# A gate unit of 512 outputs by 512 inputs in a two-layer hybrid decoder kernel

## What is computed

```python
h = rms_norm(x, norm1_g[l]) * (1.0 + sc1) + sh1
proj = h @ w_in[l]
z, xbc, dt_raw, q, k, v, gate_s, gate_a = split_cols(proj, IN_PROJ_WIDTHS)   # z: 2048 columns
# mamba2_branch: causal conv and silu of xbc, chunked scan -> y (512 tokens, 4 groups of 512)
y = y.reshape(bsz, s, SSM_D_INNER) * jax.nn.silu(z.astype(jnp.float32))
yg = y.reshape(bsz, s, SSM_GROUPS, SSM_D_INNER // SSM_GROUPS)
yg = yg * lax.rsqrt(jnp.mean(yg * yg, axis=-1, keepdims=True) + EPS)
y_ssm = (yg.reshape(...) * norm_g) @ w_ssm_out[l]
y_att = diff_attention_branch(q, k, v, ...) @ w_attn_out[l]
x = x + g1 * ((sigmoid(gate_s) * y_ssm + sigmoid(gate_a) * y_att) @ w_out[l])
x = x + g2 * (square(relu(h2 @ w_ff1[l])) @ w_ff2[l])
```

## Time and profile before

| | us |
|---|---|
| median of three runs | 2360.05 (2359.25 to 2361.26) |
| the profiled execution, its own time | 2360.11 |
| its span, first to last instruction | 2358.3 |
| TensorE matmuls busy | 2285.5 |
| VectorE busy | 1368.7 |
| ScalarE busy | 1015.1 |
| GpSimd busy | 1109.9 |

### The profile page before, as it was taken

The page is one execution under the profiler, slowest core; times in us unless marked ns, Lnnn a source line. Parts: engine busy times, 40 slices in busy tenths (PEclk is TensorE's granted clock), DMA queues, the critical chain, the costliest instruction groups (busy, mean ns, idle before and its releaser), DMA issues.

```text
span 2358.3 us, 32040 instructions
## 1 busy us (share of the span) xinstructions
PE 2285.5 (97%) x11800; PEld 1910.3 (81%) x11800; DVE 1368.7 (58%) x2041; ACT 1015.1 (43%) x1862; POOL 1109.9 (47%) x825
## 2 busy tenths in 40 slices
PE   7999998999999989999989999999999998999997
PEld 6888996887778868888878889988878786888886
DVE  7678775466653567777847777613666434321324
ACT  2566642355553232322335666533556433332322
POOL 1465643544444444444435656544444444544442
PEclk9999999999999989999999999999999998999999
DMA  6333324522224335545423333232222232233321
GB/s 253 109 95 125 103 86 155 187 78 72 71 74 153 110 131 185 189 168 204 158 92 100 118 107 108 86 98 95 71 66 70 81 116 81 99 99 98 98 94 51
DMA packets 94125, 267.19 MB, mean 113 GB/s; under 512 B 8528, under 2 KB 35536, under 8 KB 88592
## 3 DMA queue, kind: packets, MB, share of 16 engines
q1 hardware_dynamic: 84656, 248.22, 31.2%
q10 hardware_dynamic: 9312, 16.91, 2.5%
HBM read 260.77 MB, written 4.33 MB: 112 GB/s over the span
## 4 chain that ended last, share of the span: by engine, by line
PE 49%; issue 23%; POOL 10%; POOLq 10%; DVE 3%; DVEq 1%; DMA 1%; PEld 1%; ACT 1%; ACTq 1%; SPq 0%; PEldq 0%
POOL w_lo L1808 10%; PE gemm L560 10%; PE gemm L562 10%; PE gemm L561 10%; POOLq L1810 10%; PE gemm L584 3%; PE gemm L583 3%; PE gemm L585 3%; PE aux L625 2%; PE aux L804 2%; PE aux L734 2%; PE aux L842 1%; PE aux L748 1%; PE aux L743 1%; DMA ada_pe<-stream 1%
## 5 line engine op out<-in xcount | busy, mean ns | idle before, releaser
L1808 POOL TENSOR_TENSOR w_lo<-raw,w_hi 128x512 fp32r<-128x512 f32 x704 | 978.2, 1410 | 1095.3 <-ACT w_hi L934 1087.3
L934 ACT ACTIVATE w_hi<-raw 128x1024 fp32r<-128x1024 f32 x352 | 371.3, 1058 | 719.9 <-PE gemm L562 606.1
L560 PE MATMUL gemm<-h_hi,w_hi 128*128 128x512 f32 x1504 | 604.6, 402 | 5.5 <-DVE h_lo L1374 4.9
L562 PE MATMUL gemm<-h_hi,w_lo 128*128 128x512 f32 x1504 | 589.4, 392 | 0.0
L561 PE MATMUL gemm<-h_lo,w_hi 128*128 128x512 f32 x1504 | 588.4, 391 | 0.0
L560 PEld LDWEIGHTS gemm<-h_hi,w_hi 128*128 128x128 f32 x1504 | 284.5, 189 | 64.7 <-issue 9.8
L562 PEld LDWEIGHTS gemm<-h_hi,w_lo 128*128 128x128 f32 x1504 | 283.7, 189 | 61.6
L561 PEld LDWEIGHTS gemm<-h_lo,w_hi 128*128 128x128 f32 x1504 | 284.6, 189 | 57.7 <-issue 1.9
L560 PE MATMUL gemm<-op_hi,w_hi 128*128 128x512 f32 x608 | 238.6, 392 | 0.2
L562 PE MATMUL gemm<-op_hi,w_lo 128*128 128x512 f32 x608 | 236.9, 390 | 0.0
L561 PE MATMUL gemm<-op_lo,w_hi 128*128 128x512 f32 x608 | 236.7, 389 | 0.0
(11 more groups left out here) (191 smaller groups left out, 3324.5 us busy)
## 6 DMA issues: line engine op xcount, KB each, us to landing
raw<-stream SPq DMA_DIRECT2D x336, 512.0 KB
ada_late<-stream SPq DMA_DIRECT2D x30, 1024.0 KB, 4.8
seg<-decay_rows ACTq DMA_DIRECT2D x64, 256.0 KB, 3.3
ada_early<-stream SPq DMA_DIRECT2D x40, 256.0 KB, 3.9
raw<-stream SPq DMA_DIRECT2D x32, 256.0 KB
ada_first<-stream SPq DMA_DIRECT2D x5, 1024.0 KB, 20.0
x<-xT SPq DMA_DIRECT2D x2, 2048.0 KB, 10.2
ada_pe<-stream SPq DMA_DIRECT2D x3, 1024.0 KB, 14.1
```

The costliest lines, as they stand in the source:

```text
L560: mm(o, w_hi[:, slot, k, cols], hi[:, k, :], start=k == 0, stop=False)
L562: last = mm(o, w_lo[:, slot, k, cols], hi[:, k, :], start=False, stop=k == KB - 1)
L934: A(w_hi[:, slot, ks], raw[:, slot, ks], ACT.Copy).then_inc(hi_ready, 1)
L1808: gp.tensor_tensor(w_lo[:, slot, ks], raw[:, slot, ks], w_hi[:, slot, ks].bitcast(F32), ALU.subtract)
```

## The change

A gate unit becomes 512 outputs by 512 inputs. Two in a row, the early (even) and the late (odd) one, cover a group's 512 outputs and all 1024 inputs, and token block t of the group accumulates in bank t through both. A part is two k-blocks by three products, 6 matmuls of 512 columns. TensorE signals token blocks 0 to 2 with `z_done` after parts 4 to 6 of the late unit and block 3 with the unit's end. Before part 2 of the early unit it waits for banks 2 and 3 as well. ScalarE makes one tanh of a bank for each token block into one of two `zt` buffers; VectorE multiplies (tanh + 1) by the bank itself, which frees it, and then by 0.5 and y. Both stand in the tick in which TensorE runs the token block's last part (`Z_AT`): ticks 22 (block 0) and 23 (three) for group 0, 27 and 28 (two each) for group 1, 33 (four) for group 2, 37 (four) for group 3. SyncE loads a half of such a unit with two transfers, two k-blocks of each of the two 256-column units in memory. The attention gate writes its temporary into `zt[:, 0]`, with the same size.

```diff
+PART_TICK = [_tick for _tick in range(T_FIRST, T_END) for _ in range(fill_of(_tick))]
+Z_AT = {}
+for _n in range(N_Z // 2 * TB):
+    Z_AT.setdefault(PART_TICK[KB * (U_Z + 2 * (_n // TB) + 1) + TB + _n % TB], []).append(divmod(_n, TB))
...
-        zt = place("zt", [P, 2, UW], F32, r_z)
-        zh = place("zh", [P, 2, UW], F32, r_z + T2)
+        zt = place("zt", [P, 2, S], F32, r_z)
...
+                elif U_Z <= n < U_O:
+
+                    rows = slice((n - U_Z) % 2 * TB + 2 * half, (n - U_Z) % 2 * TB + 2 * half + 2)
+                    for a in range(2):
+                        sp.dma_start(raw[:, slot, TB * half + a:TB * half + TB:2],
+                                     unit_of(l, place_of(n - (n - U_Z) % 2 + a))[:, rows]).then_inc(raw_in[slot][half], 16)
...
+            def gate_tokens(l, n, part):
+
+                slot, late = n % 2, (n - U_Z) % 2
+                half, t = divmod(part, TB)
+                o = gb[t][:]
+                toks = slice(t * P, (t + 1) * P)
+                if not late and part == 2:
+                    pe.wait_ge(bank_free[1], freed_at(l, n + 1) - 2)
+                for r in range(2 * half, 2 * half + 2):
+                    k = TB * late + r
+                    hi = w_hi[:, slot, 2 * r:2 * r + 2, :].rearrange("p a n -> p (a n)")
+                    lo = w_lo[:, slot, 2 * r:2 * r + 2, :].rearrange("p a n -> p (a n)")
+                    mm(o, h_hi[:, k, toks], hi, start=k == 0, stop=False)
+                    mm(o, h_lo[:, k, toks], hi, start=False, stop=False)
+                    last = mm(o, h_hi[:, k, toks], lo, start=False, stop=k == KB - 1)
+                if t == TB - 1:
+                    last.then_inc(gemm_done, 1)
+                elif late and half:
+                    last.then_inc(S_["z_done"], 1)
...
-                def tanh_z(n, j):
-                    act.wait_ge(gemm_done, done_at(l, n))
-
-                    act.wait_ge(S_["z_used"], mid_at(l, "z_used", 2 * (n - U_Z) + j) + Z_CREDIT)
-                    src = gb[2 * (n % 2) + j][:].rearrange("p (t n) -> p t n", t=2)
-                    A(zt[:], src, ACT.Tanh, scale=0.5)
-                    A(zh[:], src, ACT.Copy, scale=0.5).then_inc(bank_free[n % 2], 1)
-                    act.drain().then_inc(S_["z_act"], 1)
+                def tanh_z(g, t):
+                    if t < TB - 1:
+                        act.wait_ge(S_["z_done"], mid_at(l, "z_done", 3 * g + t) + 1)
+                    else:
+                        act.wait_ge(gemm_done, done_at(l, U_Z + 2 * g + 1))
+
+                    act.wait_ge(S_["z_used"], mid_at(l, "z_used", TB * g + t) - 1 + Z_CREDIT)
+                    A(zt[:, t % 2], gb[t][:], ACT.Tanh, scale=0.5).then_inc(S_["z_act"], 1)
...
-                def gate_y(n, j):
-
-                    g, u = divmod(n - U_Z, 2)
-                    dve.wait_ge(S_["z_act"], mid_at(l, "z_act", 2 * (n - U_Z) + j) + 1)
-                    STT(zt[:], zt[:], 1.0, zh[:], ALU.add, ALU.mult)
+                def gate_y(g, t):
+
+                    dve.wait_ge(S_["z_act"], mid_at(l, "z_act", TB * g + t) + 1)
+                    STT(zt[:, t % 2], zt[:, t % 2], 1.0, gb[t][:], ALU.add, ALU.mult).then_inc(bank_free[t // 2], 1)
                     settle()
-                    yv = y_tok[:, g, 2 * j:2 * j + 2, u * UW:(u + 1) * UW]
-                    TT(yv, yv, zt[:], ALU.mult)
+                    yv = y_tok[:, g, t, :]
+                    STT(yv, zt[:, t % 2], 0.5, yv, ALU.mult, ALU.mult)
                     dve.drain().then_inc(S_["z_used"], 1)
```

More of the change, by code:

```diff
@@ L170 @@
     ("mid", 1, {"seed": 24, "taps": 24, "tanh": 24, "silu": 24, "decay": 32, "m": 32, "m_used": 16, "xdt": 4, "xd": 4, "dx": 4, "state": 12,
-                "z_act": 16, "z_used": 16, "y_sq": 4, "y_ms": 4, "y_rs": 4, "yn": 16, "y_hi": 16, "y_lo": 16,
+                "z_done": 12, "z_act": 16, "z_used": 16, "y_sq": 4, "y_ms": 4, "y_rs": 4, "yn": 16, "y_hi": 16, "y_lo": 16,
                 "swap": 16, "rope": 16, "v": 4, "mx": 32, "e": 32, "p": 32, "pt": 32, "o_sq": 8, "o_ms": 8, "o_rs": 8,
@@ L371, in build @@
         LO_CREDIT, DONE_CREDIT, BANK_CREDIT, AUX_CREDIT, LAYER_CREDIT = 0, 4, 2, 1, 1
-        SILU_CREDIT, U_CREDIT, ROPE_CREDIT, Z_CREDIT, OUT_CREDIT, X_CREDIT = 4, 4, 2, 1, 2, KB
+        SILU_CREDIT, U_CREDIT, ROPE_CREDIT, Z_CREDIT, OUT_CREDIT, X_CREDIT = 4, 4, 2, 2, 2, KB
         GT_CREDIT = 2
@@ L696, in mid_part @@
                         open_half(l, n, k // (KB // 2))
-                    if U_Z <= n < U_O or n == U_Q + 2 or (U_AT <= n < U_AO and AT_UNITS[n - U_AT][0] == "v"):
+                    if U_Z <= n < U_O:
+                        gate_tokens(l, n, k)
+                    elif n == U_Q + 2 or (U_AT <= n < U_AO and AT_UNITS[n - U_AT][0] == "v"):
                         unit_tokens(n % 2, k)
@@ L1146, in act_program @@
                         exp_of_dt()
-                    for j in range(2):
-                        for n in since(tick, U_Z, U_O, 1 + j):
-                            tanh_z(n, j)
+                    for g, t in Z_AT.get(tick, ()):
+                        tanh_z(g, t)
                     for g in range(GROUPS):
@@ L1620, in dve_program @@
                         steps_of_dt()
-                    for j in range(2):
-                        for n in since(tick, U_Z, U_O, 1 + j):
-                            gate_y(n, j)
+                    for g, t in Z_AT.get(tick, ()):
+                        gate_y(g, t)
                     for g in range(GROUPS):
@@ L1723, in dve_program @@
                         dve.wait_ge(gemm_done, done_at(l, U_AO + u))
-                        STT(zt[:].rearrange("p a n -> p (a n)"), gate_a[:, 2 * u + j, :], 1.0, gb[c][:], ALU.add, ALU.mult)\
+                        STT(zt[:, 0], gate_a[:, 2 * u + j, :], 1.0, gb[c][:], ALU.add, ALU.mult)\
                             .then_inc(bank_free[u % 2], 1)
                         settle()
-                        TT(mix[:, 2 * u + j, :], mix[:, 2 * u + j, :], zt[:].rearrange("p a n -> p (a n)"), ALU.add)
+                        TT(mix[:, 2 * u + j, :], mix[:, 2 * u + j, :], zt[:, 0], ALU.add)
                         dve.drain().then_inc(S_["mixed"], 1)
```

## The result

The changed kernel takes 2375.14 us (median of 4 runs, 2373.23 to 2376.02) against 2360.02 us before (4 runs, 2359.25 to 2361.26): ratio 1.0062, 95% interval 1.0045 to 1.0080, 15.1 us slower. The forecast was 2367, slower, with a range up to 2377: the sign and the main term held, and the size was less than half of what came.

A forecast was written before the change was run, and what follows sets the result against it. TensorE's stream, without slack, was taken to set the end. Columns -10.0, banks +12.4, clock +3.7, gate +5.0 and first-layer chain -4.2 sum to +6.9 us on 2360.11: 2367.0 us, range 2357 to 2377.

The forecast's parts named there:

- What bounds the kernel: From first conv unit to last y turn TensorE sets the end; a new wait there is paid in full.
- The columns, -10.0: Gate-stage parts of six 512-column matmuls replace twelve of 256: 0.078 us less per part, 128 parts, -10.0 us.
- an estimate of 2 us: Gain for the columns from the skill page's isolated-matmul formula, in place of 10; the prediction chose the measured beat.
- The banks, +12.4: Unit 12's part 2 waits 6.2 us in each layer for unit 11's banks, freed by VectorE's taps.
- The clock, +3.7: Behind each unit 12 wait TensorE's clock falls to half, costing 1.9 us a layer; bounds 0 to 4.5.
- The gate on VectorE, +5.0: Bunched gate tiles delay yn: group 1 1.2 us a layer, group 2 0.8, group 3 1.0 in the second layer.
- The first layer's chain, -4.2: Unit 21's 5.4 us wait goes, a modulation piece is read earlier; last wait ends 4.2 us sooner; bounds -6, -2.
- the 5.0 us from w_hi to the end of the next piece's reading: First layer's chain: w_hi 1.06, y_hi, y_lo and yn 0.8 each, piece 1.5, in place of 11.0 us.
- (b): Rival: it cancels, about 2360 us; the clock doesn't fall and VectorE keeps up, sum -0.2; chance 0.18.
- (c): Rival: faster, 2353.6 us; early bank release removes all first-layer waits and slow clock, 12.6 us; chance 0.12.
- (d): Rival: VectorE late at every group boundary beside POOL, 2378.6 us, sum +18.5; chance 0.12.

The follow-up runs named there:

- e1: Kernel before, with TensorE made to wait before part 2 of unit 12 until VectorE's taps have freed unit 11's banks; 2378.59 us, ratio 1.0082.
- e12: e9 with each 512-column matmul of the gate stage made as two of 256; 2352.32 us, ratio 0.9971 to the kernel before.
- e6: Changed kernel with each 512-column matmul of the gate units made as two of 256; 2377.91 us, ratio 1.0070 to the kernel before.
- e2: Changed kernel with unit 12's parts reordered, both halves of token blocks 0 and 1 first, then 2 and 3; 2361.63 us, ratio 1.0007.
- e8: Changed kernel run once more, unaltered; 2374.40 us, ratio 1.0057 to the kernel before.
- e11: Changed kernel with SyncE issuing each pair of the first layer's modulation pieces one unit later; 2365.65 us, ratio 1.0024 to the kernel before.
- e5: Changed kernel with e7's part order and the gate tiles of groups 1 to 3 spread over one tick more each; 2358.04 us, ratio 0.9992.
- e9: e5 with SyncE issuing each pair of the first layer's modulation pieces one unit later; 2344.78 us, ratio 0.9937 to the kernel before.
- e7: Changed kernel with e2's part order in the first unit of every group; 2360.85 us, ratio 1.0000 to the kernel before.
- e10: Kernel before with SyncE issuing each pair of the first layer's modulation pieces one unit later; 2346.84 us, ratio 0.9944.

## Why the prediction was right in sign and less than half in size

*What bounds the kernel.* Right: TensorE's stream sets the end, and e1 shows that a wait put into the gate stage is paid in full.

*The columns, -10.0.* The mechanism was right and the size off. In the profile it is 7.2 us by the table, 7.9 by adding up the lengths of the 122 parts that have no wait in them; e12's 7.5 and e6's 3 are net of the waits and less certain. The step between matmuls of 512 columns is 0.227 us only in a long row. In the changed kernel:

```profile
240.47 0.39 PE L611 MATMUL gemm<-w_hi,h_lo 128*128 128x512 f32 x1
...
242.74 0.39 PE L612 MATMUL gemm<-w_lo,h_hi 128*128 128x512 f32 x1
...
245.39 0.39 PE L611 MATMUL gemm<-w_hi,h_lo 128*128 128x512 f32 x1
...
247.69 0.39 PE L612 MATMUL gemm<-w_lo,h_hi 128*128 128x512 f32 x1
```

Ten steps take 2.27 us in the second and third part of a row and 2.30 behind an interruption, where single steps are 0.22 to 0.24. Of the 0.078 us counted, the first part after aux matmuls gained 0.03 (1.827 to 1.799, behind a chunk state or y offset) to 0.05 (behind a turn), the second 0.06 to 0.08. The prediction used the best part's saving for all 128.

The Trainium skill (TensorE: Matmul & The Clock Gate, Back-to-back issue gap), whose formula gave an estimate of 2 us for this term, is further off than the measured beat was: the profile shows 7.2.

*The banks, +12.4.* Right: 12.1 in the trace, one wait in each layer, of 6.04 and 6.03 us, released by the taps. e1 adds it alone and gets +18.2, e2 removes it and gets back 13. The Trainium skill (Perfetto Trace Analysis, Matmuls) advises that independent groups rotate through banks so that emptying one overlaps the next; the trace agrees, with 6.04 us of wait where that overlap was given up, and 1.11 in e2, where the other group's banks are wanted two parts later.

*The clock, +3.7.* Right in kind: 2.6 and 2.4 us in place of 1.9 a layer. It fell 4.5 and 3.9 us after the stop, not 3.1, so that more of the time at half clock had work in it. In e8 it fell 3.2 and 3.7 us after the stop, and cost 2.0 and 2.2.

*The gate on VectorE, +5.0.* The sum was near (+4.5), by other parts: group 1 cost 1.4 and 1.8 us, group 2 0.4 a layer, group 3 0.6 in the second layer. In the first layer group 3 was held to be hidden in the chain; e11 shows its 2.93 us once the chain is away. For groups 2 and 3 the cost is the bunching in program order: the operations themselves are short (0.69 us each), and with the tiles spread over more ticks the waits of these two groups are gone (e5, e9). By the medians e5 is 2.8 us below e7, with intervals that overlap. For group 1 it is not shown: spread as well, its four waits stay, 6.6 us in all in e9, and what they need is open.

*The first layer's chain, -4.2.* Named rightly (a raw load behind modulation pieces in SyncE's queue, itself behind VectorE), and the piece that the gate tile had held up was read early (at 364.62, against TensorE's own delay 8.2 us sooner). The size was off: 2.1 in this profile, 0.5 in e8. The raw load went out at 363.54, 9.0 us later than before; TensorE itself was 7.1 us later at that place, so the bunched tiles put it back by 1.9, near the 1.8 counted:

```profile
337.96 25.54 SPq L471 DMA_DIRECT2D ada_early<-stream  x10
363.54 0.97 SPq L450 DMA_DIRECT2D raw<-stream  x2
```

The term that failed is the 5.0 us from w_hi to the end of the next piece's reading. It took 7.6, from 369.23 to 376.87. GpSimd made w_lo from 370.36 to 376.31, and beside it VectorE's `yn` took 1.68 us where 0.8 was counted, and the piece 3.48 where 1.5 was:

```profile
369.23 1.06 ACT L965 ACTIVATE w_hi<-raw 128x1024 fp32r<-128x1024 f32 x1 [6.14 <-DMA raw<-stream]
370.36 2.55 POOL L1836 TENSOR_TENSOR w_lo<-raw,w_hi 128x512 fp32r<-128x512 f32 x2 [11.79 <-ACT w_hi L965]
371.78 1.68 DVE L1577 TENSOR_TENSOR yn<-y_tok,smalls 128x512 f32<-128x512 f32 x1
373.09 3.22 POOL L1836 TENSOR_TENSOR w_lo<-raw,w_hi 128x512 fp32r<-128x512 f32 x2 [0.18 <-issue]
373.39 3.48 DVE L1619 SCALAR_TENSOR_TENSOR early_acc<-ada_early,first,early_acc 128x512 f32<-128x512 f32 x2
```

So the last `yn` wait ended 2.9 us sooner against TensorE's own delay (400.16 to 404.40, with everything 7.1 later), not 4.2, and the fall of the clock behind it took 1.4 back; a shorter wait for GpSimd's queue gave 0.6. The prediction counted the fall that the chain lost, and no new one.

*Not in the sum: +3.8 in the norm stages and the end.* More time at half clock there in the profiled execution. In e8 it is 1.5. What decides it stays open.

*The rivals.* (b) needed the clock not to fall and VectorE to keep up; neither held. (c) rested on all three first-layer waits going: they go, for 13.3 us, with the queue's order (e10), and not with the bank release. (d), VectorE late at every boundary, holds for group 1 and for group 3 of the first layer: it came nearest in time (2378.6), for partly other reasons.

*The change apart from the queue.* With the queue mended on both sides, the change costs 2365.65 - 2346.84 = 18.8 us: 12.1 of bank waits, 4.3 of clock behind them, 8.1 of `yn` (9.8 against 1.7), less 7.2 of columns make 17.3. With the parts reordered and the tiles spread it gains: 2344.78 against 2346.84, 2.1 us, in ranges that overlap by little; the intervals of their ratios to before overlap, so this last gain is likely and not shown. Both kernels are faster than either of the two compared in this case, by 13 to 30 us.

## What to carry to other kernels

Where a group of work borrows banks that another engine has still to empty, first ask in which order its parts want them: moving the parts that need the borrowed banks two places back was worth 13 us, nearly twice the 7.2 us of the wider matmuls that had made them necessary. Before counting a gain on TensorE's stream, look for its waits behind other engines, for an earlier TensorE waits longer there: about 2 us of the columns' 7.2 went so, in e6 and in e12. And a DMA that has a wait in front of it holds back every load that stands behind it in the same queue: one such order cost 13.3 us here, and on TensorE it showed as waits for ScalarE, VectorE and GpSimd, never as one for that load.

## What the runs showed of the hardware

- The operation with one operand in a bank took 675 to 690 ns in all 32 cases, also in the 13 that lay wholly beside GpSimd's work, where the one with two SBUF operands had taken up to 1779.
- The prediction took a fall of the clock to need a wait longer than 2.8 us, from a single case. In the changed kernel's first layer the waits of 2.93 us (ending at 361.28) and 2.70 us (404.40) have a fall with them, that of 2.63 us (389.67) has none; windows:

```profile
357.00:372.00 15.00, 12.07 (x51) 9.68 (x51) 9.01 (x13) 3.46 (x5) 3.21 (x3) 0.89 0.52 175
...
389.00:396.00 7.00, 6.33 (x33) 5.33 (x33) 6.64 (x7) 1.47 (x3) 3.36 (x2) 1.00 0.49 138
...
404.00:410.00 6.00, 5.60 (x20) 4.56 (x21) 5.79 (x7) 0.69 (x1) 3.08 (x2) 0.72 0.19 52
```

  The two falls last some 3.4 us each (0.11 of 15 and 0.28 of 6, doubled), half as long as those at unit 12. The other runs show that the length of the wait alone does not decide: in e11 the same wait of 2.93 us (ending at 360.11) has no fall, nor has that of 2.92 in e8, and in e9 waits of 1.84 and 1.64 us (ending at 296.81 and 302.68) have one behind them:

```profile
355.00:370.00 15.00, 12.07 (x58) 9.75 (x57) 13.26 (x14) 4.25 (x6) 7.43 (x5) 1.00 0.59 177
```

```profile
300.00:310.00 10.00, 8.36 (x40) 7.02 (x40) 3.01 (x5) 4.41 (x10) 2.53 (x2) 0.83 0.00 0
```

- Two executions of the same kernel, the changed one, differed by 10 us in their time at half clock (mean 0.983 and 0.985) and by 2.7 us in all: 1.9 us less in the first 60 us and 2.3 less in the norm stages and end, 1.5 more in the first layer's chain.
